# RWKV-7 chain of a decoder step: where its masks are made, and where the next part's transposes and products are issued

## The chip, the core and the metric

The kernel runs on one core of a Trainium2 chip. The metric is the device time of one execution in microseconds. TensorE's clock has two levels, 1.2 and 2.4 GHz; the profile gives the granted clock of a stretch as a share of 2.4 GHz (0.50 is 1.2 GHz).

## The reference

One inference step of a one-layer decoder trunk for 256 prompt tokens and 8 sample tokens: one wide projection, three branches (stick-breaking attention, cross-attention to a memory, RWKV-7 time mixing), their gated sum, a norm, a mixture of 32 experts, a norm. The change touches only the RWKV-7 branch of the prompt. Its state, one 64x64 matrix for each of 8 heads, goes through all 256 tokens:

```
def step(state, inp):
    r_t, d_t, k_t, v_t, kk_t, a_t = inp
    s_a = jnp.einsum('bhvk,bhk->bhv', state, -kk_t)
    state = (state * d_t[:, :, None, :] + s_a[..., None] * (kk_t * a_t)[:, :, None, :]
             + v_t[..., None] * k_t[:, :, None, :])
    return state, jnp.einsum('bhvk,bhk->bhv', state, r_t)
wkv, y = lax.scan(step, wkv0, ...)
```

## The kernel before

One program, written out by hand for each engine; engines meet by semaphores only. SyncE and GpSimd issue DMAs, TensorE multiplies into eight PSUM banks, ScalarE (`move`) and VectorE take results out. `psum_plan` lists in order which named group of matmuls uses which bank. `start(name)` waits on TensorE until the bank's group before has been taken out, `done` says that a group is finished, `take` waits for that on the reader's side, `gone(engine, name)` waits until a group has been taken out. Every engine runs its instructions in program order.

The program has these stages, by the trace: projections, attention and memory branches to about 450 us; the RWKV chain from 486 to 671; output projections, norm and router to about 760; the experts to 1700; the last norm.

The RWKV chain works in 64-token chunks, each turned from a recurrence into products with a triangular inverse. It is cut in four parts, `it` = 0 to 3: two tiles of 128 tokens (`tt`), and in each two halves of the heads (`hh`). A part holds four 128x128 blocks (128x512 in all) and two chunks (`cc`). On TensorE a part is:

- `tab`, `tkv`: 8 transposes, moved out by ScalarE to `tokAB`, `tokKV`
- the products `g1` (two groups, 16 matmul records), `g2` (16), `g3` (8), each of 64 rows of contraction; VectorE takes them out through masks: `g1` to `Nl` (L1805) and `Nt` (L1806), `g2` and `g3` to `RB`, `AK`, `RK` (L1816 to L1819)
- `branches(...)`, steps of matmuls for the other branches' output projections and gates, 22 steps a part, spread by `PLACES`: 4 steps at "start", 2 at each other place, two places of which (U0, U1) lie in the state steps. A group of such steps that is complete is moved out by ScalarE, and of the memory branch gated and summed by GpSimd (`gated`, L650, L651)
- a wait for `T_ready`, that VectorE gives after L1809 to L1812: `Tm` and `Tt` are the first level's mask of `Nl`, `Nt`, plus the identity
- five levels of the inverse: `X` = N'T, moved out by ScalarE; then `TX` and `XT`, which VectorE adds to `Tm` (L1824) and `Tt` (L1827). N' is `Nt` times the level's mask; GpSimd makes all five `Nm[lv]` at the part's start (L674), as soon as both `g1` are taken out
- `MV`, `Z`, `WT`, moved out by ScalarE
- the state steps, for each of two chunks: `U`, added by VectorE (L1837), `dS`, added to the state (L1840) and decayed (L1843) by VectorE, which gives `S_ready` for the next `U`
- `Y`, the part's output, moved out by ScalarE.

All of one part stands ahead of all of the next on every engine. On VectorE a part's order is: g1 masks, T, g2 and g3 masks, levels, state steps. After the four parts come norm, gate and output projection of the branch (L1848 to L1872), and `merged`. The experts' weights come in 192 chunks of 2 MB through six buffers (`pair_loads`): the first six are asked for when the buffers' last users (the last gate, `o`, `merged`, `res`) are done, each later one when TensorE has used the chunk before it in its buffer.

Of the kernel before, what the change touches and what calls it, by code (L numbers as in the profile page):

```python
# [21 lines left out]
P = 128  # L22
# [31 lines left out]
Q0, K0, V0, MQ0, RW0 = 0, 4, 8, 12, 16  # L54

# [15 lines left out]
def beside():  # L71

    g = []
    for kind, br in (("gate", 0), ("o", 0), ("gate", 1), ("o", 1), ("gate", 2)):
# [6 lines left out]
PLACES = {"start": (0, 4), "X0": (4, 6), "X1": (6, 8), "X2": (8, 10), "X3": (10, 12), "X4": (12, 14),  # L81
          "MV": (14, 16), "WT": (16, 18), "U0": (18, 20), "U1": (20, 22)}
# [18 lines left out]
def psum_plan():  # L101
# [61 lines left out]
    for tt in range(2):  # L163
        for hh in range(2):
            n = (tt, hh)
            add(("tab",) + n, six[4])
            add(("tkv",) + n, six[5])
            for hp in range(2):
                add(("g1", hp) + n, six[hp])
            for hp in range(2):  # L170
                add(("g2", hp) + n, six[2 + hp])
            for hp in range(2):
                add(("g3", hp) + n, six[4 + hp])
            for lv in range(5):
                add(("X", lv) + n, six[0])
                if lv < 4:
                    add(("TX", lv) + n, six[1])
                add(("XT", lv) + n, six[2])
            add(("MV",) + n, six[3])
            add(("Z",) + n, six[4])  # L180
            add(("WT",) + n, six[5])
            for cc in range(2):
                add(("U", cc) + n, six[0])
                add(("dS", cc) + n, six[1])
            add(("Y",) + n, six[3])
# [46 lines left out]
def build(nc, A, O):  # L232
# [6 lines left out]
    with ctx:  # L239
# [89 lines left out]
        tokAB, tokKV = ar(R0, 2, 256), ar(R0 + 512, 2, 256)  # L329
        Nl, Nt, Tm, Tt, Xm, AK, RB, RK = (ar(R0 + 1024 + 512 * i, 4, P) for i in range(8))  # L330
        Nm = [ar(R0 + 5120 + 512 * i, 4, P) for i in range(5)]
# [194 lines left out]
        def _(g):  # L526
# [57 lines left out]
            link(g.tensor_tensor(m_lo[:], blk[:], m_upi[:], ALU.subtract))  # L584
            link(g.tensor_scalar(blk64[:], blk[:], 1.0 / 64, 0.0, ALU.mult, ALU.add))
# [83 lines left out]
            for it in range(4):  # L669
                n = (it // 2, it % 2)  # L670
                gone(g, ("g1", 0) + n)
                gone(g, ("g1", 1) + n)
                for lv in range(5):
# [39 lines left out]
        def _(pe):  # L713
# [307 lines left out]
            for tt in range(2):  # L1021
                for hh in range(2):
                    n = (tt, hh)
                    cols = slice(tt * P, tt * P + P)
                    it = 2 * tt + hh
                    tiles = (2 * hh, 2 * hh + 1)
                    if it == 0:
                        pe.wait_ge(sem("hats"), 1)
                    for nm, srcs in (("tab", (KK, AA)), ("tkv", (KM, pT[:, 24:28, :]))):
                        b = start((nm,) + n)  # L1030
                        for i, src in enumerate(srcs):
                            for tl, t in enumerate(tiles):
                                last = tr(b[:, 256 * i + P * tl:256 * i + P * tl + P], src[:, t, cols])
                        done((nm,) + n, last)
                    hats = {"A": KK, "B": AA, "K": KM, "R": pT[:, RW0:RW0 + 4, :]}
                    for nm, prods in (("g1", ("BA", "AB")), ("g2", ("BR", "KA")), ("g3", ("KR",))):
                        for hp in range(2):
                            b = start((nm, hp) + n)
                            rows = slice(64 * hp, 64 * hp + 64)
                            for i, lr in enumerate(prods):  # L1040
                                for tl, t in enumerate(tiles):
                                    c0 = 256 * i + P * tl
                                    last = mm(b[:, c0:c0 + P], hats[lr[0]][rows, t, cols], hats[lr[1]][rows, t, cols], True, True)
                            done((nm, hp) + n, last)

                    branches(*at_place(it, "start"))
                    pe.wait_ge(sem("T_ready"), it + 1)
                    for lv in range(5):
                        if lv:
                            gone(pe, ("TX", lv - 1) + n)  # L1050
                        pe.wait_ge(sem("Nm_ready"), 5 * it + lv + 1)
                        b = start(("X", lv) + n)
                        for u in range(4):
                            last = mm(b[:, u * P:u * P + P], Nm[lv][:, u, :], Tm[:, u, :], True, True)
                        done(("X", lv) + n, last)
                        branches(*at_place(it, f"X{lv}"))
                        if lv:
                            gone(pe, ("XT", lv - 1) + n)
                        gone(pe, ("X", lv) + n)
                        if lv < 4:  # L1060
                            b = start(("TX", lv) + n)
                            for u in range(4):
                                last = mm(b[:, u * P:u * P + P], Tt[:, u, :], Xm[:, u, :], True, True)
                            done(("TX", lv) + n, last)
                        b = start(("XT", lv) + n)
                        for u in range(4):
                            last = mm(b[:, u * P:u * P + P], Xm[:, u, :], Tt[:, u, :], True, True)
                        done(("XT", lv) + n, last)
                    b = start(("MV",) + n)
                    gone(pe, ("tkv",) + n)  # L1070
                    for hp in range(2):
                        gone(pe, ("g2", hp) + n)
                        gone(pe, ("g3", hp) + n)
                    for tl in range(2):
                        for hp in range(2):
                            u, c0 = 2 * hp + tl, 64 * (2 * tl + hp)
                            last = mm(b[:, c0:c0 + 64], AK[:, u, :], tokKV[:, 1, c0:c0 + 64], True, True)
                    done(("MV",) + n, last)
                    branches(*at_place(it, "MV"))
                    gone(pe, ("MV",) + n)  # L1080
                    gone(pe, ("XT", 4) + n)
                    b = start(("Z",) + n)
                    for tl in range(2):
                        for hp in range(2):
                            u, j = 2 * hp + tl, 2 * tl + hp
                            last = mm(b[:, 64 * j:64 * j + 64], Tt[:, u, :], MVs[:, j, :], True, True)
                    done(("Z",) + n, last)
                    b = start(("WT",) + n)
                    for tl in range(2):
                        for hp in range(2):  # L1090
                            u, c0 = 2 * hp + tl, 64 * (2 * tl + hp)
                            last = mm(b[64 * hp:64 * hp + 64, P * tl:P * tl + P], tokAB[:, 0, c0:c0 + 64], Tt[:, u, :], True, True)
                    done(("WT",) + n, last)
                    branches(*at_place(it, "WT"))
                    gone(pe, ("WT",) + n)
                    gone(pe, ("tab",) + n)
                    for cc in range(2):
                        c = 2 * tt + cc
                        rows = slice(64 * cc, 64 * cc + 64)
                        if 2 * it + cc:  # L1100
                            pe.wait_ge(sem("S_ready"), 2 * it + cc)
                        else:
                            pe.wait_ge(sem("S_zero"), 1)
                        b = start(("U", cc) + n)
                        for tl, t in enumerate(tiles):
                            last = mm(b[rows, P * tl:P * tl + P], WTs[:, tl, rows], Sb[c % 3][:, t, :], True, True)
                        done(("U", cc) + n, last)
                        branches(*at_place(it, f"U{cc}"))
                        gone(pe, ("U", cc) + n)
                        b = start(("dS", cc) + n)  # L1110
                        for tl in range(2):
                            o = b[:, P * tl:P * tl + P]
                            uc = Us.rearrange("p a b -> p (a b)")[rows, P * tl:P * tl + P]
# [964 lines left out]
```

## Time and profile before

| | |
|---|---|
| three runs | 1732.66, 1735.74, 1736.46 us |
| median | 1735.74 us |
| the profiled execution | 1734.74 us, its span 1733.1 us |
| TensorE matmuls busy | 1538.8 us, 89% |
| VectorE busy | 596.8 us, 34% |
| ScalarE, GpSimd busy | 280.2 us, 180.5 us |
| granted clock, mean | 0.939 |
| HBM read | 528.91 MB |

The profile is one execution. Its timeline merges neighbouring instructions of one engine and form; the idle time ahead of an instruction and what ended it stand in brackets. Matmuls are pipelined and their ends are modelled, so work is better measured from start to start. A float32 matmul of the program is two matmul records. PE is TensorE, DVE VectorE, ACT ScalarE, POOL GpSimd.

### The profile page before, as it was taken

The numbers are of one execution on the slowest core, as the hardware profiler recorded it, in microseconds if no ns is written. First come the engines' busy times: TensorE is split into PE (matmuls) and PEld (weight loads), VectorE is DVE, ScalarE is ACT, GpSimd is POOL, SyncE is SP. The second block draws the span as 40 slices with busy tenths as digits, with TensorE's granted clock in tenths as the row PEclk, the third lists the DMA queues.
The fourth block names the chain that finished last, engine by engine and source line by source line (L and its number), as shares of the span: only waits on it lengthen the run. The fifth ranks groups of instructions, "written<-read, shape, count | busy, mean of one in ns | idle before, by whom it ended". The sixth has DMA issues, their size and how long they took to land.

```text
span 1733.1 us, 20943 instructions
## 1 busy us (share of the span) xinstructions
PE 1538.8 (89%) x7762; PEld 818.1 (47%) x7762; DVE 596.8 (34%) x888; ACT 280.2 (16%) x538; POOL 180.5 (10%) x290
## 2 busy tenths in 40 slices
PE   7985877778898997969999999999999999999993
PEld 5764533456687775454343434443434333333331
DVE  2699633157634444422121212121212121212125
ACT  1100233113311112110111111111111111011102
POOL 5522131103033112000000000000000000000000
PEclk9998878889988998969999999999999999999997
DMA  8798796766211012439999999999999999999990
GB/s 306 249 326 317 234 306 217 279 249 205 98 25 46 4 50 81 194 126 425 425 429 429 428 428 429 429 429 428 426 429 429 429 429 427 428 429 429 429 425 27
DMA packets 83913, 534.10 MB, mean 308 GB/s; under 512 B 8639, under 2 KB 9722, under 8 KB 59282
## 3 DMA queue, kind: packets, MB, share of 16 engines
q1 hardware_dynamic: 69714, 487.61, 68.7%
q0 software_dynamic: 14144, 45.79, 8.1%
q8 instruction: 31, 0.51, 0.1%
q14 instruction: 24, 0.20, 0.0%
HBM read 528.91 MB, written 4.46 MB: 308 GB/s over the span
## 4 chain that ended last, share of the span: by engine, by line
PE 56%; DMA 26%; DVE 9%; issue 4%; ACT 2%; POOL 1%; POOLq 0%; SPq 0%; DVEq 0%; ACTq 0%
PE bank L728 54%; DMA projT<-in_w_gate_up 23%; PE bank L729 2%; DVE ring L1604 2%; DMA ring<-in_w_in 2%; DMA ring<-in_w_mem_kv 1%; DVE ring L1693 1%; DVE sample_logits L1610 1%; DVE arena L1695 0%; DMA ring<-in_cache_sb_k 0%; DVE arena L1810 0%; DVE arena L1812 0%; DVE arena L1811 0%; ACT arena L1355 0%; DVE arena L2041 0%
## 5 line engine op out<-in xcount | busy, mean ns | idle before, releaser
L728 PE MATMUL bank<-arena 128*128 128x128 f32 (+9 forms) x2172 | 346.4, 364 | 36.9 <-DVE arena L1812 11.2
L728 PEld LDWEIGHTS bank<-arena 128*128 128x128 f32 (+4 forms) x2172 | 238.2, 187 | 153.3 <-issue 127.3
L728 PE MATMUL bank<-ring,memT 128*64 128x512 f32 (+2 forms) x1152 | 282.8, 599 | 8.7 <-ACT memT L1550 7.6
L728 PE MATMUL bank<-projT,ring 128*128 128x264 f32 x1056 | 264.5, 407 | 26.2 <-DMA ring<-in_w_in 17.3
L1981 DVE TENSOR_SCALAR arena<-bank 128x256 f32<-128x256 f32 x64 | 27.0, 422 | 637.6 <-PE bank L728 637.6
L728 PE MATMUL bank<-projT 128*64 128x512 f32 (+1 forms) x1056 | 235.4, 591 | 8.6 <-DMA projT<-in_w_gate_up 8.6
L728 PEld LDWEIGHTS bank<-projT,ring 128*128 128x128 f32 x1056 | 206.3, 200 | 73.0 <-issue 21.6
L728 PE MATMUL bank<-ring,projT 128*64 128x512 f32 x1024 | 230.3, 597 | 0.0
L728 PEld LDWEIGHTS bank<-ring,memT 128*64 128x64 f32 (+2 forms) x1152 | 85.2, 139 | 156.6 <-issue 138.5
L728 PEld LDWEIGHTS bank<-projT 128*64 128x64 f32 (+1 forms) x1056 | 77.1, 141 | 162.2 <-issue 136.8
L728 PEld LDWEIGHTS bank<-ring,projT 128*64 128x64 f32 x1024 | 69.3, 137 | 147.4 <-issue 147.4
L707 POOL DMA_DIRECT2D out_y_sample<-arena x1 | 0.5, 507 | 966.6 <-DVE arena L1892 966.6
L1546 ACT ACTIVATE arena<-arena 128x256 f32<-128x256 f32 x64 | 26.7, 417 | 419.1 <-DVE arena L1981 419.1
L729 PE MATMUL bank<-ident,arena 128*128 128x128 f32 (+4 forms) x386 | 71.3, 304 | 22.9 <-DMA arena<-in_x_sample 8.1
L729 PEld LDWEIGHTS bank<-ident,arena 128*128 128x128 f32 (+4 forms) x386 | 51.7, 171 | 80.0 <-issue 67.0
L1604 DVE TENSOR_TENSOR ring<-ring,bank 128x4096 f32<-128x4096 f32 x16 | 70.6, 4414 | 40.1 <-PE bank L728 20.3
L1355 ACT ACTIVATE arena<-bank 128x512 f32<-128x512 f32 (+7 forms) x98 | 48.0, 513 | 222.9 <-PE bank L728 178.8
L1610 DVE TENSOR_REDUCE sample_logits<-ring 128x64 f32<-128x4096 f32 x16 | 70.7, 4420 | 0.6
L1355 ACT ACTIVATE projT<-bank 128x264 f32<-128x264 f32 (+2 forms) x68 | 26.0, 384 | 239.9 <-PE bank L728 228.4
L1996 DVE TENSOR_TENSOR arena<-arena,bank 128x512 f32<-128x512 f32 x64 | 41.1, 683 | 56.3 <-PE bank L728 56.3
L448 POOL DMA_DIRECT2D ring<-in_cache_sb_k x64 | 34.4, 538 | 109.2 <-issue 89.8
L448 POOL DMA_DIRECT2D ring<-in_cache_sb_v x64 | 34.4, 537 | 94.6 <-issue 94.6
(272 smaller groups left out, 974.0 us busy)
## 6 DMA issues: line engine op xcount, KB each, us to landing
ring<-in_w_gate_up SPq DMA_DIRECT2D x64, 2048.0 KB, 21.2
projT<-in_w_gate_up SPq DMA_DIRECT2D x64, 2048.0 KB, 23.8
ring<-in_w_down SPq DMA_DIRECT2D x64, 2048.0 KB, 20.4
ring<-in_w_in SPq DMA_DIRECT2D x13, 2048.0 KB, 9.1
ring<-in_cache_sb_k SPq DMA_DIRECT2D x64, 256.0 KB, 5.2
ring<-in_cache_sb_k POOLq DMA_DIRECT2D x64, 256.0 KB, 5.9
ring<-in_cache_sb_v SPq DMA_DIRECT2D x64, 256.0 KB, 5.0
ring<-in_cache_sb_v POOLq DMA_DIRECT2D x64, 256.0 KB, 5.3
```

The lines of the kernel that those rows point to most:

```text
L448: eng.dma_start(dst[:, j, :], src[bass.ds(page, 1), :, :].rearrange("g p n -> p (g n)")).then_inc(sem(landed_sem), 16)
L707: g.dma_start(dst, yacc[0:rows, tt, :]).then_inc(sem("out_done"), 16)
L728: mm = lambda out, l, r, first, last, **k: pe.matmul(out, l, r, start=first, stop=last, **k)
L729: tr = lambda out, src, rows=P: pe.transpose(out, src, ident[0:rows, 0:rows])
L1355: act.activation(dst, src_of(b), func, **k).then_inc(freed_by(name), 1)
L1546: act.activation(sg[u % 2], gb[u % 2], ACT.Sigmoid, scale=SWA).then_inc(sem("sg_ready"), 1)
L1604: prod_ = tt_(k, k, q[:, :].unsqueeze(1).to_broadcast([P, 8, W5]), ALU.mult)
L1610: v.tensor_reduce(zs[:, b_, 8 * half:8 * half + 8, :], slot(name).rearrange("p (n h d) -> p n h d", n=8, h=SBH), AX.X, ALU.add).then_inc(s ...
L1693: tt_(k, k, q[:, :].unsqueeze(1).to_broadcast([P, 2, W5]), ALU.mult).then_inc(freed_by(("mqb", b_)), 1)
L1981: ts(g_, chunk[:, 0:512:2], LIMIT, None, ALU.min).then_inc(sem("g_ready"), 1)
L1996: tt_(yacc[:, tt, c], yacc[:, tt, c], bank[b][:, :], ALU.add).then_inc(sem("scatter_added"), 1)
```

## The change

- GpSimd no longer makes `Nm`. VectorE does (`next_level`), one level ahead: level 0's right after `T_ready`, level lv+1's ahead of the TX addition of level lv. Two buffers instead of five.
- `m_lo` is multiplied once by the first level's mask (one more GpSimd instruction of 128x128 among the masks), so that g1's second half goes to `Tm` directly; `Nl` and L1809 go.
- The next part's transposes and its `g1` and `g2` are issued on TensorE between this part's state steps: tab, tkv behind U0, g1 behind dS0, g2 behind U1 and dS1. Only `g3` stays at the part's own start. `tokAB`, `tokKV`, `RB`, `RK` get second buffers, taken in turn.
- ScalarE moves the next part's transposes out ahead of this part's Y.
- VectorE does the next part's g1 masks and T (`first_blocks`) between its addition to U1 and the second state update (`decay_state(1)`); the g2 and g3 masks (`other_products`) come after it.
- The branch steps at U0 and U1 go to "start", which has 8 instead of 4. Banks: g1 in banks 2 and 4, g2 in 5 and 6, g3 in 2 and 4, Y in bank 0.

```diff
-PLACES = {"start": (0, 4), "X0": (4, 6), "X1": (6, 8), "X2": (8, 10), "X3": (10, 12), "X4": (12, 14),
-          "MV": (14, 16), "WT": (16, 18), "U0": (18, 20), "U1": (20, 22)}
+PLACES = {"start": (0, 8), "X0": (8, 10), "X1": (10, 12), "X2": (12, 14), "X3": (14, 16), "X4": (16, 18),
+          "MV": (18, 20), "WT": (20, 22)}
...
+            link(g.tensor_tensor(m_lo[:], m_lo[:], lev[0][:], ALU.mult))
...
-                gone(g, ("g1", 0) + n)
-                gone(g, ("g1", 1) + n)
-                for lv in range(5):
-                    g.tensor_tensor(Nm[lv], Nt, lev[lv + 1][:].unsqueeze(1).to_broadcast([P, 4, P]),
-                                    ALU.mult).then_inc(sem("Nm_ready"), 1)
...
+                ahead = RW_PARTS[it + 1] if it < 3 else None
+                state_in_chunk(0)
+                if ahead:
+                    turned_hats(ahead, "tab")
+                    turned_hats(ahead, "tkv")
+                state_change(0)
+                if ahead:
+                    gram(ahead, "g1", 0)
+                    gram(ahead, "g1", 1)
+                state_in_chunk(1)
+                if ahead:
+                    gram(ahead, "g2", 0)
+                state_change(1)
+                if ahead:
+                    gram(ahead, "g2", 1)
...
+            def next_level(it, lv):
+
+                tt_(Nm[lv % 2], Nt, m4(lev[lv + 1]), ALU.mult).then_inc(sem("Nm_ready"), 1)
...
-                tt_(Tm, Nl, m4(lev[0]), ALU.mult)
                 link(tt_(Tt, Nt, m4(lev[0]), ALU.mult))
                 tt_(Tm, Tm, m4(ident), ALU.add)
                 tt_(Tt, Tt, m4(ident), ALU.add).then_inc(sem("T_ready"), 1)
+                next_level(it, 0)
...
                 for lv in range(5):
                     if lv < 4:
+                        next_level(it, lv + 1)
                         b = take(v, ("TX", lv) + n)
...
+                    if cc == 0:
+                        decay_state(0)
+                if it < 3:
+                    first_blocks(it + 1)
+                decay_state(1)
```

## Rows read from the trace of the kernel before

**Rows 1.** The page, its 40 slices: GB/s moved in each slice of 43.3 us
```profile
GB/s 306 249 326 317 234 306 217 279 249 205 98 25 46 4 50 81 194 126 425 425 429 429 428 428 429 429 429 428 426 429 429 429 429 427 428 429 429 429 425 27
```

**Rows 2.** The chain of waits, ahead of part 3's first level: start us, us, what
```profile
628.68 1.64 DVE arena L1811
630.32 1.68 DVE arena L1812
```

**Rows 3.** Timeline of TensorE, U0 of part 2 to X0 of part 3: start, length, instruction, [idle]
```profile
613.56 0.65 PE L728 MATMUL bank<-arena 128*64 128x128 f32 x4
614.14 1.16 PE L728 MATMUL bank<-projT,ring 128*128 128x264 f32 x4
615.23 1.16 PE L728 MATMUL bank<-arena 64*128 64x128 f32 x8
617.36 0.65 PE L728 MATMUL bank<-arena 128*64 128x128 f32 x4 [0.98 <-DVE arena L1843]
...
622.48 0.88 PE L729 MATMUL bank<-ident,arena 128*128 128x128 f32 x6
...
623.50 1.37 PE L728 MATMUL bank<-arena 64*128 64x128 f32 x13
...
626.70 2.05 PE L728 MATMUL bank<-projT,ring 128*128 128x264 f32 x8
632.04 2.07 PE L728 MATMUL bank<-arena 128*128 128x128 f32 x8 [3.30 <-DVE arena L1812]
```

**Rows 4.** Busy time by stretches: length, engines' busy us, clock (PEclk is the column after POOL)
```profile
520.88:544.40 23.52, 18.84 (x113) 14.91 (x113) 10.57 (x17) 2.36 (x5) 7.20 (x6) 0.76 0.00 1
544.40:569.65 25.25, 25.25 (x164) 22.39 (x164) 8.61 (x17) 4.92 (x10) 6.73 (x8) 0.89 0.24 84
...
588.14:613.56 25.42, 25.42 (x165) 22.62 (x165) 8.61 (x17) 4.53 (x9) 2.31 (x2) 0.88 0.00 1
...
632.04:656.27 24.23, 24.23 (x165) 21.36 (x165) 8.61 (x17) 4.93 (x10) 2.31 (x2) 0.93 0.00 1
656.27:665.20 8.93, 7.95 (x58) 6.00 (x57) 3.03 (x8) 0.39 (x1) 0.00 (x0) 1.00 0.01 2
```

**Rows 5.** Timeline of TensorE, X0 of part 0
```profile
498.17 1.16 PE L728 MATMUL bank<-arena 128*128 128x128 f32 x8 [1.30 <-DVE arena L1812]
```

**Rows 6.** Busy time by stretches of 2 us; the clock is the column after POOL
```profile
528.00:530.00 2.00, 2.00 (x10) 1.78 (x10) 0.52 (x2) 0.00 (x0) 0.00 (x0) 0.50 0.00 0
...
576.00:578.00 2.00, 2.00 (x21) 1.57 (x19) 0.85 (x2) 0.00 (x0) 0.00 (x0) 1.00 0.00 0
...
580.00:582.00 2.00, 2.00 (x30) 2.00 (x30) 1.14 (x4) 0.35 (x1) 0.00 (x0) 1.00 0.04 8
...
588.00:590.00 2.00, 1.86 (x8) 1.86 (x9) 2.00 (x7) 0.00 (x0) 2.00 (x2) 0.50 0.00 0
...
594.00:596.00 2.00, 2.00 (x17) 1.97 (x17) 1.17 (x2) 0.11 (x1) 0.00 (x0) 0.91 0.00 0
```

**Rows 7.** Timeline of VectorE: a level's addition, U's addition, masks
```profile
505.15 0.69 DVE L1824 TENSOR_TENSOR arena<-arena,bank 128x512 f32<-128x512 f32 x1 [2.29 <-PE bank L728]
...
618.12 0.43 DVE L1837 TENSOR_TENSOR arena<-bank,arena 64x256 f32<-64x256 f32 x1 [0.29 <-PE bank L728]
...
626.28 0.69 DVE L1809 TENSOR_TENSOR arena<-arena,lev 128x512 f32<-128x512 f32 x1
...
631.91 0.41 DVE L1816 TENSOR_TENSOR arena<-bank,m_upi 128x256 f32<-128x256 f32 x1
632.24 0.41 DVE L1817 TENSOR_TENSOR arena<-bank,m_up 128x256 f32<-128x256 f32 x1
```

**Rows 8.** Timeline of GpSimd: a gated sum of the memory branch
```profile
504.58 0.75 POOL L650 TENSOR_TENSOR projT<-sample_logits,projT 128x264 f32<-128x264 f32 x1 [2.57 <-ACT sample_logits L1355]
```

**Rows 9.** Timeline of GpSimd: the mask m_lo, among the setup instructions
```profile
60.57 0.46 POOL L584 TENSOR_TENSOR m_lo<-blk,m_upi 128x128 f32<-128x128 f32 x1
```

**Rows 10.** The chain of waits behind GpSimd's masks: the K pages' transfer
```profile
80.89 7.08 DMA ring<-in_cache_sb_k
```

More of the change, by code:

```diff
@@ L162, in psum_plan, with grams @@
             turn += 1
[L163 to L173, printed above, removed]
-            for lv in range(5):
[L175 to L185, printed above, removed]
+    def grams(n):
+        add(("tab",) + n, six[4])
+        add(("tkv",) + n, six[5])
+        for hp in range(2):
+            add(("g1", hp) + n, six[2 + hp])
+        for hp in range(2):
+            add(("g2", hp) + n, six[4 + hp])
+    grams(RW_PARTS[0])
+    for it, n in enumerate(RW_PARTS):
+        for hp in range(2):
+            add(("g3", hp) + n, six[2 + hp])
+        for lv in range(5):
+            add(("X", lv) + n, six[0])
+            if lv < 4:
+                add(("TX", lv) + n, six[1])
+            add(("XT", lv) + n, six[2])
+        add(("MV",) + n, six[3])
+        add(("Z",) + n, six[4])
+        add(("WT",) + n, six[5])
+        if it < 3:
+            grams(RW_PARTS[it + 1])
+        for cc in range(2):
+            add(("U", cc) + n, six[0])
+            add(("dS", cc) + n, six[1])
+        add(("Y",) + n, six[0])
     add("wkv_out", 0)
@@ new lines, in _, with turned_hats, gram @@
+            hats = {"A": KK, "B": AA, "K": KM, "R": pT[:, RW0:RW0 + 4, :]}
+            def turned_hats(n, nm):
+                tt, hh = n
+                b = start((nm,) + n)
+                for i, src in enumerate({"tab": (KK, AA), "tkv": (KM, pT[:, 24:28, :])}[nm]):
+                    for tl in range(2):
+                        last = tr(b[:, 256 * i + P * tl:256 * i + P * tl + P], src[:, 2 * hh + tl, tt * P:tt * P + P])
+                done((nm,) + n, last)
+            def gram(n, nm, hp):
+                tt, hh = n
+                cols = slice(tt * P, tt * P + P)
+                b = start((nm, hp) + n)
+                rows = slice(64 * hp, 64 * hp + 64)
+                for i, lr in enumerate({"g1": ("BA", "AB"), "g2": ("BR", "KA"), "g3": ("KR",)}[nm]):
+                    for tl in range(2):
+                        c0 = 256 * i + P * tl
+                        last = mm(b[:, c0:c0 + P], hats[lr[0]][rows, 2 * hh + tl, cols], hats[lr[1]][rows, 2 * hh + tl, cols], True, True)
+                done((nm, hp) + n, last)
@@ L1097, in _ @@
                     for cc in range(2):
                         c = 2 * tt + cc
[L1099 to L1113, printed above, removed]
-                            mm(o, tokAB[rows, 1, P * tl:P * tl + P], uc, True, False)
-                            last = mm(o, tokKV[rows, 0, P * tl:P * tl + P], tokKV[rows, 1, P * tl:P * tl + P], False, True)
@@ L1128, in _ @@
-                    done(("Y",) + n, last)
+                        mm(b[:, P * tl + 64 * cc:P * tl + 64 * cc + 64], Sb[c % 3][:, t, :],
+                           pT[:, RW0 + t, c * C:c * C + C], cc == 0, True, skip_group_check=True)
+                    for hp in range(2):
+                        u, j = 2 * hp + tl, 2 * tl + hp
+                        o = b[64 * hp:64 * hp + 64, P * tl:P * tl + P]
+                        mm(o, Us[:, j, :], RB[:, u, :], False, True, skip_group_check=True)
+                        last = mm(o, tokKV[:, 1, 64 * j:64 * j + 64], RK[:, u, :], False, True, skip_group_check=True)
@@ L1129, in _ @@
+                done(("Y",) + n, last)
             pe.wait_ge(sem("S_ready"), 8)
@@ L1485, in _, with turned_hats @@
             act.wait_ge(sem("arena_clear"), 2)
[L1486 to L1490 removed]
+            def turned_hats(it):
+                for nm, dst in (("tab", tokABs), ("tkv", tokKVs)):
+                    move((nm,) + RW_PARTS[it], dst[it % 2].rearrange("p a b -> p (a b)"), lambda b: b[:, :])
+            turned_hats(0)
+            for it, n in enumerate(RW_PARTS):
+                tt, hh = n
                 beside_moves(it, "start")
@@ L1797, in _, with first_blocks @@
             m4 = lambda m: m[:].unsqueeze(1).to_broadcast([P, 4, P])
-            for it in range(4):
-                tt, hh = it // 2, it % 2
-                n = (tt, hh)
-                part = lambda b, i: b[:, 256 * i:256 * i + 256].rearrange("p (a b) -> p a b", a=2)
+            part = lambda b, i: b[:, 256 * i:256 * i + 256].rearrange("p (a b) -> p a b", a=2)
+            def next_level(it, lv):
+                tt_(Nm[lv % 2], Nt, m4(lev[lv + 1]), ALU.mult).then_inc(sem("Nm_ready"), 1)
+            def first_blocks(it):
+                n = RW_PARTS[it]
                 for hp in range(2):
```

218 lines of the change are left out of this document (112 added, 106 removed).

## The prediction

> **What bounds the kernel now.** I read the page first, then the chain of waits, then each engine's timeline over the RWKV chain, and last short windows with the clock. The page's line of GB/s [rows 1] shows two kinds of stage: from about 780 us to the end the transfers run flat near 428 GB/s (the experts), before that they don't. The expert stage starts its reloads when TensorE uses a chunk, and each of its first six chunks is asked for when a TensorE or VectorE step ahead of it is done (code of `pair_loads`), so whatever brings the RWKV chain forward should bring the end forward by as much. In the chain of waits around a part's start [rows 2] the path runs through VectorE's two additions of the identity, 1.64 and 1.68 us, and then TensorE's X0.
>
> TensorE's timeline from one part's first state step to the next part's first level [rows 3] shows what is queued: U0 at 613.56, 2 steps of branch matmuls, dS0, U1 after 0.98 us of idle time for the state, the same again, Y, transposes at 622.48, products at 623.50, 4 branch steps at 626.70, and 3.30 us of idle time before X0 at 632.04. The same by stages with the clock [rows 4]: first level to first state step takes 25.25, 25.42 and 24.23 us in parts 1 to 3. In part 0 it takes 22.71 us (498.17 [rows 5] to 520.88 [rows 4]) for the same instructions. The difference (2.5, 2.7, 1.5 us) is clock: right after the 3.3 us of idle time the granted clock is at 0.50, the 1.2 GHz level, and at 594 to 596 is back at 0.91 [rows 6]. So VectorE's preparation costs twice, by idle time and by the slow matmuls behind it.
>
> **Part by part.**
>
> *Transposes, products, branch steps.* Nothing of them is added or dropped (22 branch steps a part as before, now 8 ahead of X0 and none behind U0, U1). What counts is TensorE's own work from U0 to the next X0, at full clock from starts in [rows 3]: U 614.14 - 613.56 = 0.58, twice 1.16; dS: 617.36 - 0.98 - 0.06 of latency - 615.23 = 1.09, twice 2.18; Y: 622.48 - (617.36 + 0.58 + 1.09 + 1.09) = 2.36; transposes 1.02; the five kinds of products 626.70 - 623.50 = 3.20; 8 branch steps 2 x 2.05 = 4.10. Sum 14.02 us. If nothing waits, a part takes 22.71 + 14.02 = 36.73 us, against 43.74 (25.25 from 544.40, 18.49 to 588.14) and 43.90 (25.42 + 18.48) [rows 4].
>
> *Does anything wait?* Count from U0. Transposes end at 1.60. VectorE's addition to U begins 0.76 after the U matmuls begin and takes 0.43 [rows 7], done at 1.2, so dS0 goes at 1.60 and ends at 2.69. VectorE's two state steps and their waits took 1.04 us; S_ready is at 3.73, while the g1 products (16 of the 40 records, 1.28) keep TensorE until 3.97: U1 isn't late, by 0.24. g2 of half a head pair (0.64) ends at 5.19, U's second addition at 5.2: dS1 is on time. Then g2, Y until 9.28. VectorE starts the first blocks at 5.2: four masks at 0.33 [rows 7], then three operations of 128x512 at 0.69 and the first level mask at 0.69: 9.3 with latencies. The second state step follows to 10.2, the six other products (0.33 each) to 12.2, the next level mask to 12.9. X0 is due on TensorE at 14.02, its inputs are there 4.7 us earlier, and its bank (0, now also Y's) is moved out by ScalarE behind Y, while TensorE runs g3 and the branch steps. The decay of chunk 1 now waits behind `first_blocks` on VectorE, but the state it makes is asked for by the next U0, 27 us later, and its bank by TX0, behind X0. The three idle times and the clock loss all go; late next is TensorE itself.
>
> *Masks.* The 20 GpSimd multiplications go, 16 of 20 new ones on VectorE lie inside levels. There VectorE idles 2.29 us before the TX addition [rows 7]. Alone an operation of this shape takes 0.69; beside GpSimd's masks the same shape took 1.64 and 1.68 [rows 2]. GpSimd keeps its gated sums (0.75 each [rows 8]), so I bound the new mask at 0.69 to 1.7 us: below 2.29 either way, cost nothing. The TX addition, which reads PSUM, took 0.69 while GpSimd was busy with such a sum (505.15 [rows 7] against 504.58 to 505.33 [rows 8]), so it stays. The Trainium skill ("SBUF — State Buffer", on the shared port pair) says a VectorE operation with two SBUF inputs is shut out by a GpSimd one that reads SBUF, for a whole instruction, and one with a single SBUF input isn't. The trace agrees with both halves (1.64 against 0.69; 0.69 unmoved). By that rule the new masks can be held for one sum, 0.75 us, which the same idle time covers.
>
> *Part 0's start.* Its X0 comes after 8 instead of 4 branch steps. TensorE had 1.30 us of idle time there [rows 5]; 2.05 us more work brings X0 from 498.17 to 498.92: 0.75 us lost. It gets back below.
>
> *The end of part 3* has no next part to fill in, and U0, U1 have lost their branch steps. U0 0.58, dS0 at 1.24, ends at 2.33, U1 at 3.37, dS1 at 4.61, Y 5.70 to 8.06, against 8.93 [rows 4]: 0.87 gained, and 24.23 - 22.71 = 1.52 of clock ahead of it.
>
> *One GpSimd instruction early on* (m_lo times lev0, about 60 us). Its neighbour took 0.46 [rows 9], 0.52 with its link, and GpSimd's chain there ends in the K page transfers for which VectorE waited (chain of waits, [rows 10]): 0.52 lost, bounds 0 and 0.6.
>
> *Sum.* Part 0: 46.23 (22.71 + 23.52) - 36.73 - 0.75 = 8.75. Part 1: 7.01. Part 2: 7.17. Part 3: 2.39. Together 25.32, less 0.52: 24.8 us. The profiled execution took 1734.74 us (span 1733.1), 1.0 below the median of the three runs: 1709.9 for a like execution, 1711 for the median.
>
> **Rivals.**
>
> *A, the clock falls in the new stretch.* Against the gain speaks part 0 of before: the clock went to 0.50 at 526 and stayed there with TensorE busy 2.00 of 2.00 us (528 to 530, [rows 6]), through dS, Y, transposes and products; U0 to X0 took 23.52 there against 18.49 later. For it speaks the same work at 1.00 at 576 to 578 and 580 to 582 [rows 6], with fewer gaps ahead, and after the change there are none. If it falls once in a boundary, it costs what part 0 shows, 23.52 - 18.49 = 5.0: one boundary gives 1716, three give 1726. The end of part 3 alone, with 2.3 us of idle time in 6, can lose 1.5 to 4: 1713 to 1715. The Trainium skill ("TensorE: Matmul & The Clock Gate", the clock gate) says the default is the slow clock and activity releases it. By that the gapless stretch stays at 2.4 GHz, the forecast; the busy stretch at 528 at 0.50 doesn't agree at once with it.
>
> *B, slower.* The same mechanism carried through: the transposes, 64-row products and state steps in a row hold the clock at 1.2 GHz from U0 to X0 at all three boundaries. Each costs 14.02 more; 42 - 25 makes the kernel 17 us slower, 1736 + 17 = about 1753. It decides at 25.3 / 3 = 8.4 us of full-speed work run at half clock in each boundary. Against it: the rows at 576 and 580, of such work, at 1.00 [rows 6].
>
> *C, no change:* the experts' transfers set the end whatever the chain does. Then 1735 to 1736. Against it: these transfers are asked for by the steps that move.
>
> *D, the overlap fails in part:* U1 waits for the state (slack only 0.24 us) or dS1 for its addition, say 0.5 us each and three times: 1712 to 1714. This lies in the forecast's own range; a full failure (only the masks move, so that 3 x 1 us of slow additions a part go, 12 us with some clock) gives 1722.
>
> **How the numbers follow.** Forecast (1706 to 1716) 0.68; A 0.17; D's full failure 0.05; C 0.04; B 0.06. The range 1705 to 1720 takes in one or two fallen clocks and 2 us each way for the spread of the runs (1732.66 to 1736.46), and leaves out about 2 in 10. About 0.2% (3.5 us) is what a measurement of this kernel can tell from no change. Faster 0.90, same 0.04, slower 0.06.
>
> **What would show it.** Right: no idle time of TensorE ahead of X0 in parts 1 to 3, X0 to X0 near 36.7 us, clock 1.00 from the first X0 to the last U0, the mask lines at 0.69 to 1.7 us ahead of TX additions that still wait for TensorE. Wrong: U1 or dS1 with idle time from VectorE, clock rows at 0.50 between U0 and X0, TX0 waiting for a mask, or an unchanged start of the experts' reloads at an earlier end of the chain.

## The result, and the profile after

The changed kernel took 1710.34 us (median of 4 runs, 1704.75 to 1714.96) against 1736.10 us (4 runs, 1732.66 to 1736.59) for the kernel before: ratio 0.9862, 95% interval 0.9836 to 0.9888. A second set gave 1716.03 us (6 runs, 1707.45 to 1720.16) against 1734.05 us (12 runs, 1723.44 to 1739.21): 0.9882, 0.9862 to 0.9902. So it is 18 to 26 us faster; the forecast was 1711.

| | before | after |
|---|---|---|
| profiled execution | 1734.74 us | 1706.75 us |
| span | 1733.1 us | 1705.0 us |
| TensorE matmuls busy | 1538.8 us | 1527.2 us |
| VectorE busy | 596.8 us | 595.3 us |
| GpSimd busy | 180.5 us | 149.3 us |
| mean granted clock | 0.939 | 0.944 |

First the stretches that answer to [rows 4]: first level to first state step, then first state step to the next part's first level, for parts 0 and 1; then the levels of part 3, and its tail, from U0 to the end of Y. The columns are those of [rows 4]; the clock stands behind POOL.

```profile
493.97:516.30 22.33, 22.33 (x165) 19.80 (x163) 9.31 (x14) 5.71 (x12) 6.49 (x9) 1.00 0.01 1
516.30:530.34 14.04, 14.04 (x114) 12.17 (x114) 10.07 (x23) 2.25 (x5) 1.80 (x3) 1.00 0.00 0
530.34:552.66 22.32, 22.32 (x165) 19.80 (x163) 8.74 (x14) 4.92 (x10) 2.96 (x5) 1.00 0.25 95
552.66:566.70 14.04, 14.04 (x114) 12.17 (x113) 9.62 (x23) 1.86 (x4) 0.00 (x0) 1.00 0.01 1
603.06:625.39 22.33, 22.33 (x165) 19.80 (x163) 8.75 (x14) 4.53 (x9) 0.00 (x0) 1.00 0.00 1
625.39:635.44 10.05, 7.91 (x49) 6.16 (x48) 3.02 (x8) 0.39 (x1) 0.00 (x0) 0.77 0.01 2
```

TensorE is busy all of the first five stretches, at clock 1.00. A part takes 36.36 us (22.32 + 14.04) where it took 43.74 and 43.90. Only the last row has idle time (10.05 - 7.91) and a clock below 1.

The stretch from U0 to X0 of part 1 on TensorE, which answers to [rows 3]:

```profile
516.30 0.65 PE L728 MATMUL bank<-arena 128*64 128x128 f32 x4
516.88 0.87 PE L729 MATMUL bank<-ident,arena 128*128 128x128 f32 x6
...
520.44 0.65 PE L728 MATMUL bank<-arena 128*64 128x128 f32 x4
...
526.67 3.83 PE L728 MATMUL bank<-projT,ring 128*128 128x264 f32 x16
530.34 1.05 PE L728 MATMUL bank<-arena 128*128 128x128 f32 x8
```

and on VectorE, from the first state update to the TX addition of level 1 (L1890 is the decay that ends a state update, L1900 the addition to U, L1850 and L1851 the additions of the identity, L1837 the new level mask, L1876 and L1879 the additions of TX and XT):

```profile
519.55 0.42 DVE L1890 TENSOR_TENSOR arena<-arena 128x256 f32<-128x256 f32 x1
...
521.20 0.43 DVE L1900 TENSOR_TENSOR arena<-bank,arena 64x256 f32<-64x256 f32 x1 [0.70 <-PE bank L728]
...
523.90 0.69 DVE L1850 TENSOR_TENSOR arena<-arena,ident 128x512 f32<-128x512 f32 x1
524.51 0.68 DVE L1851 TENSOR_TENSOR arena<-arena,ident 128x512 f32<-128x512 f32 x1
525.11 0.68 DVE L1837 TENSOR_TENSOR arena<-arena,lev 128x512 f32<-128x512 f32 x1
...
528.62 1.13 DVE L1837 TENSOR_TENSOR arena<-arena,lev 128x512 f32<-128x512 f32 x1
533.27 0.69 DVE L1876 TENSOR_TENSOR arena<-arena,bank 128x512 f32<-128x512 f32 x1 [3.52 <-PE bank L728]
534.24 0.69 DVE L1879 TENSOR_TENSOR arena<-arena,bank 128x512 f32<-128x512 f32 x1 [0.28 <-PE bank L728]
534.96 0.69 DVE L1837 TENSOR_TENSOR arena<-arena,lev 128x512 f32<-128x512 f32 x1
537.07 0.69 DVE L1876 TENSOR_TENSOR arena<-arena,bank 128x512 f32<-128x512 f32 x1 [1.42 <-PE bank L728]
```

The first mask is done at 525.79, 9.5 us behind U0, and X0 starts at 530.34. The additions of the identity take 0.69 and 0.68 us instead of 1.64 and 1.68 [rows 2]. In a level the mask takes 0.69 us out of VectorE's idle time (2.29 [rows 7], now 1.42 left). U1, the row at 520.44, has no idle time ahead of it: its state was done at 519.97. One mask, at 528.62, ran beside two gated sums of GpSimd and took 1.13 us; nobody waited for it.

The tail of part 3 on TensorE, and the clock there in stretches of 2 us:

```profile
625.39 0.65 PE L728 MATMUL bank<-arena 128*64 128x128 f32 x4
626.62 1.16 PE L728 MATMUL bank<-arena 64*128 64x128 f32 x8 [0.58 <-DVE arena L1900]
628.75 0.65 PE L728 MATMUL bank<-arena 128*64 128x128 f32 x4 [0.97 <-DVE arena L1890]
629.99 1.36 PE L728 MATMUL bank<-arena 64*128 64x128 f32 x8 [0.59 <-DVE arena L1900]
...
636.14 1.09 PE L729 MATMUL bank<-ident,arena 128*128 128x128 f32 x4 [0.58 <-ACT arena L1386]
```

```profile
628.00:630.00 2.00, 0.66 (x5) 0.42 (x5) 1.57 (x5) 0.00 (x0) 0.00 (x0) 1.00 0.00 0
630.00:632.00 2.00, 2.00 (x12) 1.77 (x12) 0.58 (x2) 0.00 (x0) 0.00 (x0) 0.70 0.04 8
632.00:634.00 2.00, 2.00 (x13) 1.55 (x13) 0.27 (x1) 0.00 (x0) 0.00 (x0) 0.50 0.00 0
638.00:640.00 2.00, 2.00 (x6) 1.59 (x5) 0.95 (x3) 1.17 (x1) 1.31 (x2) 0.50 0.19 33
```

Three gaps, two of which branch steps used to fill (the one of 0.97, the wait for the state, was there before), then the clock at 0.50 while Y and the first norm products run. The last row of TensorE is a wait that I had not counted: the transposes of `wkv_out` use bank 0, which now also holds Y, and wait 0.58 us until ScalarE has moved Y out.

**A yardstick.** Runs of one kernel lie up to 21 us apart, too wide for terms of 1 to 5 us. The traces are steadier. I measure from X0 of part 0 to the start of the residual's products, the first that need the whole merged tensor. Those rows of TensorE's timeline, before and after:

```profile
702.67 17.55 PE L728 MATMUL bank<-ring,memT 128*8 128x512 f32 x64 [1.12 <-DVEq L1872]
```

```profile
674.86 17.55 PE L728 MATMUL bank<-ring,memT 128*8 128x512 f32 x64 [1.12 <-DVEq L1934]
```

| kernel | X0, part 0 | residual | between | gain | X0 to X0, parts 0, 1, 2 | residual to the span's end |
|---|---|---|---|---|---|---|
| before | 498.17 | 702.67 | 204.50 | | 46.23, 43.74, 43.90 | 1030.4 |
| after | 493.97 | 674.86 | 180.89 | 23.6 | 36.37, 36.36, 36.36 | 1030.1 |
| after, second set | 505.53 | 687.06 | 181.53 | 23.0 | 36.37, 36.37, 36.37 | 1031.3 |
| masks alone | 502.24 | 689.47 | 187.23 | 17.3 | 42.89, 37.85, 37.85 | 1030.5 |
| overlap alone | 503.50 | 685.86 | 182.36 | 22.1 | 36.99, 36.65, 36.65 | 1030.4 |
| tail filled | 502.42 | 680.54 | 178.12 | 26.4 | 36.38, 36.36, 36.37 | 1030.7 |
| steps behind | 497.03 | 669.81 | 172.78 | 31.7 | 34.60, 34.59, 34.59 | 1030.6 |
| no start steps | 497.62 | 669.28 | 171.66 | 32.8 | 34.73, 32.80, 32.82 | 1030.4 |
| overlap and a tiny op | 498.95 | 679.84 | 180.89 | 23.6 | 36.36, 36.37, 36.36 | 1031.1 |

The last column settles one rival: whatever the chain does, the rest takes 1030.1 to 1031.3 us behind it.

The yardstick leaves out part 0's start, where the change costs time. From the first transpose to the residual's products the kernel before took 216.17 us (from 486.50), the changed one 193.64 and 196.24 (from 481.22 and 490.82), the masks alone 196.66 (from 492.81) and the overlap alone 197.04 (from 488.82). Counted so, the gains are 22.5 and 19.9 us for the whole change, 19.5 for the masks alone and 19.1 for the overlap alone. These carry an error that the yardstick hasn't: the granted clock rises from 0.50 to 1.00 within this start, about 9 us behind its beginning before, 6 with the masks alone, 10 and 13 in the two traces of the changed kernel, and the 2.6 us between these two come mostly from that.

### The profile page after: what moved, and what is told of

The parts are those of the page before. It is cut to its first block, busy times and chain, and to the rows that moved or that the text cites. A ratio compares the mean times of both kernels' runs of the same rounds, so it can differ in the third digit from the quotient of the medians.

```text
span 1705.0 us, 20920 instructions
## 1 busy us (share of the span) xinstructions
PE 1527.2 (90%) x7762; PEld 810.9 (48%) x7762; DVE 595.3 (35%) x904; ACT 279.8 (16%) x538; POOL 149.3 (9%) x271
## 4 chain that ended last, share of the span: by engine, by line
PE 58%; DMA 28%; DVE 7%; issue 4%; ACT 2%; POOL 1%; POOLq 0%; SPq 0%; DVEq 0%; ACTq 0%
PE bank L728 56%; DMA projT<-in_w_gate_up 24%; PE bank L729 2%; DMA ring<-in_w_in 2%; DVE ring L1639 1%; DMA ring<-in_cache_sb_k 1%; DMA ring<-in_w_mem_kv 1%; DVE ring L1728 1%; DVE sample_logits L1645 1%; DVE arena L1730 1%; ACT arena L1386 0%; DVE arena L2103 0%; POOLq L452 0%; POOL arena L610 0%; ACT L1427 0%
## 5 line engine op out<-in xcount | busy, mean ns | idle before, releaser
L728 PE MATMUL bank<-arena 128*128 128x128 f32 (+9 forms) x2172 | 335.3, 358 | 23.3 <-DVE arena L1681 8.7
L728 PEld LDWEIGHTS bank<-arena 128*128 128x128 f32 (+4 forms) x2172 | 230.2, 182 | 134.2 <-issue 123.2
L453 POOL DMA_DIRECT2D ring<-in_cache_sb_k x64 | 34.6, 540 | 109.9 <-issue 89.1
L453 POOL DMA_DIRECT2D ring<-in_cache_sb_v x64 | 34.6, 541 | 86.9 <-issue 86.9
```

Source lines behind the costliest of these rows:

```text
L453: eng.dma_start(dst[:, j, :], src[bass.ds(page, 1), :, :].rearrange("g p n -> p (g n)")).then_inc(sem(landed_sem), 16)
L728: mm = lambda out, l, r, first, last, **k: pe.matmul(out, l, r, start=first, stop=last, **k)
```

## Experiments

**The changed kernel again.** No edit.

> The changed kernel itself once more, to see its spread (four runs lay between 1704.75 and 1714.96 us) and a second trace. Theory: the gain is fixed in the RWKV chain, X0 to X0 36.4 us in parts 0 to 3, and the spread comes from ahead of it (the profiled execution reached the chain's first X0 at 493.97 us, before's at 498.17, while the change can only make that 0.75 later): about 1710, same distances inside the chain. Rival: the spread comes from the chain, from a clock that falls in some executions between U0 and X0; then X0 to X0 differs from 36.4 us in a second trace of another total.

1716.03 us. Its chain is the same to 0.01 us a part, with total spans of 1705.0 and 1718.4; X0 of part 0 came at 493.97 and at 505.53. The spread lies ahead of the chain, in code that the change touches by one GpSimd instruction. What moves it there was not followed. The yardstick differs by 0.64 us, nearly all of it behind the last X0: the clock fell again in the tail, but earlier, behind the second of the three gaps (0.97 us, to 640.33) and not behind the third:

```profile
640.00:642.00 2.00, 1.09 (x5) 0.69 (x5) 1.18 (x4) 0.00 (x0) 0.00 (x0) 0.61 0.00 0
```

**Masks alone**, in the kernel before:

```diff
+            link(g.tensor_tensor(m_lo[:], m_lo[:], lev[0][:], ALU.mult))
...
-                for lv in range(5):
-                    g.tensor_tensor(Nm[lv], Nt, lev[lv + 1][:].unsqueeze(1).to_broadcast([P, 4, P]),
...
-                tt_(Tm, Nl, m4(lev[0]), ALU.mult)
...
+                tt_(Nm[0], Nt, m4(lev[1]), ALU.mult).then_inc(sem("Nm_ready"), 1)
...
+                        tt_(Nm[lv + 1], Nt, m4(lev[lv + 2]), ALU.mult).then_inc(sem("Nm_ready"), 1)
```

> The kernel before with the masks alone: VectorE makes them a level ahead, m_lo already has the first level's mask; transposes, products and branch steps stay where they were. Theory (the two halves of the change remove the same idle time and the same clock loss): T is ready 3.0 us sooner, the idle time ahead of X0 falls from 3.30 to about 0.3 us, the clock stays at 1.00 behind it; 5.6 us in each of parts 1 and 2, 3 in part 0 (its clock loss in the state steps stays), 1.5 in part 3, 1.3 at part 0's start, less 0.5: about 1719 to 1720 us. Rival (the halves add, each has its own price): 3 us a part and no clock, 12 us less 0.5: about 1724 us, with clock rows at 0.50 behind X0 as before.

1719.53 us (4 runs; ratio 0.9903, 0.9883 to 0.9924), beside 1734.05 for the kernel before and 1716.03 for the changed one. That is the first theory's number; the rival's gain of 11.5 us (a ratio of 0.9934) lies just outside the interval, and the trace decides. TensorE at X0 of part 1 and part 2, and the stretches from U0 of part 0 and from X0 of part 1:

```profile
545.13 1.13 PE L723 MATMUL bank<-arena 128*128 128x128 f32 x8 [0.26 <-issue]
...
582.98 1.13 PE L723 MATMUL bank<-arena 128*128 128x128 f32 x8 [0.26 <-issue]
```

```profile
524.65:545.13 20.48, 18.85 (x113) 14.94 (x113) 7.53 (x17) 2.36 (x5) 2.00 (x3) 0.75 0.00 0
545.13:567.53 22.40, 22.40 (x164) 19.88 (x164) 11.22 (x21) 4.92 (x10) 4.24 (x6) 1.00 0.25 95
567.53:582.98 15.45, 14.21 (x113) 11.38 (x113) 7.13 (x17) 2.03 (x5) 0.00 (x0) 1.00 0.01 1
```

0.26 us of idle time instead of 3.30, and levels at clock 1.00 where they had 0.88 or 0.89. Part 0's fall in the state steps stays (0.75), as expected. On the yardstick 17.3 of the 23.6 us are there with the masks alone; with part 0's start counted, 19.5 of 19.9 to 22.5, for here that start got shorter (9.43 us instead of 11.67 from the first transpose to X0, in part by a clock that rose earlier), and in the changed kernel longer. By the medians of this set it is 14.5 of 18.0 us.

**Overlap alone**, in the changed kernel, with GpSimd's five masks at the part's start:

```diff
+        Nm += [x[:].rearrange("p (a b) -> p a b", a=4) for x in (w_lora, w_gate2, m_page)]
...
+                for lv in range(5):
+                    g.tensor_tensor(Nm[lv], Nt, lev[lv + 1][:].unsqueeze(1).to_broadcast([P, 4, P]),
+                                    ALU.mult).then_inc(sem("Nm_ready"), 1)
...
-                next_level(it, 0)
...
-                        next_level(it, lv + 1)
```

> The changed kernel, but GpSimd makes all five level masks at the part's start as before (three of the five buffers lie in w_lora, w_gate2s and m_page, which nothing uses by then). Theory: VectorE's three operations of 128x512 in the first blocks cost 1 us more each beside GpSimd, T is ready about 11.7 us behind U0 instead of 8.7, the first mask at about 8.3, and X0 is due only at 14.0: nothing waits, the time is that of the changed kernel, within 2 us. Rival (the halves add): the masks bring 12 of the 25 us, so this one takes about 1722 us and shows idle time ahead of X0.

1716.35 us (4 runs; 0.9874, 0.9845 to 0.9902), 0.3 us from the changed kernel in the same set, on the yardstick 22.1 us. VectorE's first blocks of part 1:

```profile
533.33 0.69 DVE L1851 TENSOR_TENSOR arena<-arena,lev 128x512 f32<-128x512 f32 x1
534.06 1.64 DVE L1852 TENSOR_TENSOR arena<-arena,ident 128x512 f32<-128x512 f32 x1
535.62 1.75 DVE L1853 TENSOR_TENSOR arena<-arena,ident 128x512 f32<-128x512 f32 x1
...
543.50 0.69 DVE L1876 TENSOR_TENSOR arena<-arena,bank 128x512 f32<-128x512 f32 x1 [2.60 <-PE bank L734]
544.39 0.69 DVE L1879 TENSOR_TENSOR arena<-arena,bank 128x512 f32<-128x512 f32 x1 [0.21 <-PE bank L734]
547.37 0.69 DVE L1876 TENSOR_TENSOR arena<-arena,bank 128x512 f32<-128x512 f32 x1 [2.29 <-PE bank L734]
```

The slow additions are back, and X0 of part 1, at 540.49, doesn't wait for them: T is ready at 537.4. So 17.3 + 22.1 is far above 23.6: either half removes nearly the same idle time and clock loss.

**Tail filled**, in the changed kernel:

```diff
+                else:
+                    branches(TAIL, TAIL + 2)
                 state_change(0)
...
-            branches(248, 256)
+            branches(TAIL + 6, 256)
...
-    add("wkv_out", 0)
+    add("wkv_out", 6)
```

> The changed kernel with 6 of the last 8 branch steps moved from behind the chain into part 3's state steps (two behind U0, two behind dS0, two behind U1), and wkv_out in bank 6 instead of 0. In the changed kernel U0 to Y's end took 10.05 us there, with 0.58, 0.97 and 0.59 us of idle time and the clock at 0.50 from 631 to 641, and wkv_out waited 0.58 us for Y's bank. Theory (gaps bring the clock down): no gap, the clock stays at 1.00, U0 to Y's end takes 9.0 us, the first norm products come 1 us sooner and run at full speed: 4 us less, about 1706. Rival (the narrow matmuls of Y and dS bring it down by themselves): the clock falls all the same, gain below 1.5 us.

1711.28 us (4 runs; 0.9858, 0.9839 to 0.9878). The stretches of part 3, its levels and from U0 to Y's end; then two short ones, right behind 1.91 us of idle time between the norm's products, and in the long idle time behind them:

```profile
611.53:633.86 22.33, 22.33 (x165) 19.80 (x163) 8.75 (x14) 4.53 (x9) 0.00 (x0) 1.00 0.00 1
633.86:642.82 8.96, 8.96 (x61) 6.67 (x61) 3.03 (x8) 0.39 (x1) 0.00 (x0) 1.00 0.01 2
...
648.00:650.00 2.00, 2.00 (x11) 1.71 (x10) 0.00 (x0) 1.73 (x4) 0.00 (x0) 1.00 0.00 0
655.00:657.00 2.00, 0.00 (x0) 0.00 (x0) 1.96 (x1) 0.00 (x0) 0.00 (x0) 0.50 0.92 393
```

More work in less time: 8.96 us where 10.05 stood. The same Y and dS, without gaps, ran at 1.00: the narrow matmuls by themselves don't bring the clock down. The filling also put wide matmuls between them, but those aren't needed for it: from U0 to g3 the changed kernel has none (516.30 to 526.67), and that stretch ran at 1.00. Nor does a gap always bring it down: 1.91 us between the wide matmuls of the norm left it at 1.00 (648 to 650). What fell was the clock of narrow matmuls with gaps among them, and not behind each such gap (see the last section).

The runs took 4.75 us less than the changed kernel's in the same set; the yardstick gains 2.8 us (3.4 against the second trace), where I had expected 4. From U0 to the norm's second products 3.6 us were there (13.66 instead of 17.28 us). TensorE then had 11.4 instead of 8.8 us of idle time, and the output projection started at the slow clock as before and stayed there longer: from its start to the residual's products it took 18.64 instead of 17.81 us, 0.8 lost again.

**Steps behind**: the tail filled, and 4 instead of 8 steps ahead of X0; 18 steps instead of 8 behind the norm's last product, and GpSimd gates the sums that they complete there too.

```diff
+PLACES = {"start": (0, 4), "X0": (4, 6), "X1": (6, 8), "X2": (8, 10), "X3": (10, 12), "X4": (12, 14),
+          "MV": (14, 16), "WT": (16, 18)}
...
-GROUP_FIRST, GROUP_STEP = 160, 22
+GROUP_FIRST, GROUP_STEP = 160, 18
...
+TAIL = 232
```

> The kernel with part 3's gaps filled, and 4 instead of 8 branch steps ahead of each X0; the 18 steps left over stand behind the norm's last product (there were 8 in the changed kernel), where TensorE had 8.8 us of idle time and then the branch's output projection at the 1.2 GHz level. Theory (TensorE's own work bounds a part, its inputs at X0 are ready 4.7 us early): X0 to X0 34.3 us in parts 0 to 3 instead of 36.4, no idle time ahead of X0; 8.2 us less in four parts for 6 steps more in the tail that replace its gaps; from the first X0 to the end of the output projection's products 165.9 - 8.2 - up to 2 (clock) = 156 to 158 us, against 168.7 in the changed kernel: the time about 11 us below the changed kernel's. Rival (VectorE bounds X0 once the cover goes): X0 to X0 stays near 36 us with idle time ahead of X0.

1703.12 us (5 runs; 0.9824, 0.9794 to 0.9855). Levels 22.33 us as before, U0 to X0 12.26 instead of 14.04, no idle time at X0. Mine had been 34.3 a part, 34.6 came: I had priced four steps at 2.05 us, the length of their row in [rows 3] (from the first matmul's start to the last one's end, which is more than from start to start); in a row they cost 1.78 (14.04 - 12.26). For that reason and since the clock still fell behind the steps, the yardstick says 172.8, 8.1 below the changed kernel's and not 11.

**No start steps**: as above with none ahead of X0 (14 a part, 34 behind).

```diff
+PLACES = {"start": (0, 0), "X0": (0, 2), "X1": (2, 4), "X2": (4, 6), "X3": (6, 8), "X4": (8, 10),
+          "MV": (10, 12), "WT": (12, 14)}
...
+GROUP_FIRST, GROUP_STEP = 160, 14
...
+TAIL = 216
```

> As the run with the steps behind, but no branch step at all ahead of X0 (14 a part, 34 behind the norm's last product). It measures how much cover X0 has. Theory (from the changed kernel's trace: the first level mask is done 9.5 us behind U0, TensorE gets to X0 at 10.4): still no idle time ahead of X0, X0 to X0 about 32.3 to 32.5 us, at most 0.2 us of waiting for the first TX addition, which stands behind the other six masks; behind the chain the 34 steps take 17.4 us where 12 were idle, so the total is that of the run with the steps behind or up to 3 us above it. Rival (the 4.7 us of cover were not there): idle time of 1 us or more ahead of X0 in each part and a clock at 0.50 behind it, X0 to X0 above 34 us.

1700.18 us (4 runs; 0.9804, 0.9777 to 0.9832). TensorE over part 1, and VectorE at its first level:

```profile
532.35:554.78 22.43, 22.43 (x166) 19.91 (x165) 11.38 (x21) 5.32 (x11) 4.47 (x6) 1.00 0.01 1
554.78:565.15 10.37, 10.37 (x97) 9.02 (x96) 6.99 (x17) 1.86 (x4) 1.49 (x2) 1.00 0.00 0
```

```profile
530.79 0.69 DVE L1845 TENSOR_TENSOR arena<-arena,lev 128x512 f32<-128x512 f32 x1
...
534.30 0.68 DVE L1845 TENSOR_TENSOR arena<-arena,lev 128x512 f32<-128x512 f32 x1
535.39 0.69 DVE L1884 TENSOR_TENSOR arena<-arena,bank 128x512 f32<-128x512 f32 x1 [0.41 <-PE bank L730]
```

U0 to X0 is 10.37 us and still free of waits: the first mask was done at 531.48, 0.9 us ahead of X0 at 532.35, and the TX addition still waits for TensorE, 0.41 us. The cover in the changed kernel was 4.5 us (525.79 to 530.34), where the prediction had counted 4.7. Parts 1 and 2 are 32.8 us long, 0.3 over the forecast. Part 0 is not: it took 34.73 us, because its levels ran partly at the slow clock:

```profile
497.62:521.98 24.36, 24.36 (x165) 21.69 (x165) 11.74 (x21) 5.32 (x11) 4.47 (x6) 0.91 0.00 1
```

With no steps ahead of it X0 came while the clock was still at 0.50, and nearly 2 us of the saving went there (24.36 instead of 22.43 us). The median of the runs is 2.9 us below that of the steps behind, inside the intervals; the yardstick says 1.1.

**No start steps, again:**

> The kernel without branch steps ahead of X0 once more, for an interval beside the kernel before: its chain from the first X0 to the residual's products took 171.7 us against 204.5 before. Theory: ratio 0.981, 32 to 33 us below before. Rival: the last look was a lucky one, 0.985 or above.

1702.47 us (5 runs) against 1731.71 (9 runs): 0.9826, 0.9800 to 0.9852; yardstick 671.62 - 499.96 = 171.66, as in the first trace. It beats the kernel before by its interval and the changed kernel by the yardstick (171.66 against 180.89); between it and the version with 4 steps the runs can't tell.

**Overlap alone, and a tiny VectorE operation in each level:**

```diff
                     if lv < 4:
+                        v.memset(ar(19200, 4), 0.0)
                         b = take(v, ("TX", lv) + n)
```

> The kernel with the overlap alone (GpSimd's masks), plus one tiny VectorE memset (4 elements a row) in each of the first four levels, where the changed kernel has its mask. The levels took 3.80 us each in the changed kernel and with the masks alone, 3.87 us before and with the overlap alone; TensorE's gap ahead of the next X was 0.16 against 0.23 us. Theory: VectorE has two waits ahead of its TX addition (the last addition taken out, TX full), and with an instruction between them each instruction carries one, so that the addition starts 0.07 us sooner: 3.80 us a level here too, the parts 0.3 us shorter than with the overlap alone. Rival: it is GpSimd's work or the place of the buffers: 3.87 us stays.

One run, 1712.51 us. VectorE in a level:

```profile
543.77 0.06 DVE L1875 MEMSET arena<- 128x4 f32 x1
545.85 0.69 DVE L1877 TENSOR_TENSOR arena<-arena,bank 128x512 f32<-128x512 f32 x1 [2.02 <-PE bank L734]
...
547.57 0.06 DVE L1875 MEMSET arena<- 128x4 f32 x1
549.65 0.69 DVE L1877 TENSOR_TENSOR arena<-arena,bank 128x512 f32<-128x512 f32 x1 [2.02 <-PE bank L734]
```

A level takes 3.80 us (549.65 - 545.85), with the overlap alone 3.87 (547.37 - 543.50 above). The whole yardstick is 180.89 us, to the hundredth that of the changed kernel. The rival (GpSimd's work, or the place of the buffers) is refuted. So in this one trace, once the overlap is there, who makes the masks is worth nothing; what the masks still brought was this instruction's place.

## Why the prediction was right, step by step

*What bounds.* Right. TensorE's own work is the limit from U0 to X0: taking 4 and 8 branch steps out shortened it from 14.04 to 12.26 and 10.37 us, without idle time. The rest of the program followed the chain.

*Levels.* I took 22.71 us for every part. 22.33 came: 0.38 less in each of four parts, 1.5 in all. It is the 0.07 us a level above, and 0.10 where X0 begins a part.

*U0 to X0.* 14.02 forecast, 14.04 measured, and that closeness is luck. The 8 branch steps took 3.67 us (526.67 to 530.34) instead of 4.10, and all the rest took 10.37 instead of 9.92, as the run without start steps shows again. The price of the products is what was low: [rows 3] has their 40 records one behind the other in 3.20 us, and the new order pulls them apart. A likely reason, not tested, is that products which contract different halves of the rows start side by side when they are neighbours (pairs at 540.95 and 541.06 in the trace of the masks alone), while the records of one group come 0.11 us apart. There was no wait at U1: its state was done at 519.97, 0.47 us ahead of U1 at 520.44, more than the 0.24 that were counted. At dS1 there was no idle time either, but U's addition was done only at 521.63, when dS1 was due.

*Masks at no cost.* Right, 0.69 us and once 1.13 inside my bounds of 0.69 to 1.7, always ahead of an addition that waits for TensorE. The Trainium skill ("SBUF — State Buffer", "Who interferes with whom") says that a VectorE instruction with two SBUF inputs contends with a GpSimd one that reads SBUF. The overlap alone agrees with it again, 1.64 and 1.75 us beside GpSimd's masks against 0.69 and 0.68 without them.

*Part 0's start.* From the first transpose to X0 took 11.67 us before (486.50 to 498.17), 12.75 after (481.22 to 493.97), 14.71 in the second trace (490.82 to 505.53), where the branch steps ran longer at the slow clock. 0.75 forecast, 1.1 and 3.0 measured: the sign was right and the size depends on when the clock comes back.

*The end of part 3* is the mis-sized term. Forecast: 0.87 gained behind U0 and 1.52 ahead of it. Ahead, 1.90 came (24.23 - 22.33). Behind, from U0 to the residual's products, 46.40 us (656.27 to 702.67) became 49.47 (625.39 to 674.86): 3.1 lost instead of 0.9 gained, 4.0 off. The step that failed is "Y 5.70 to 8.06", which had the idle time right (the gaps were 0.58, 0.97 and 0.59, as worked out) but the matmuls behind it at full clock, and left out the bank of `wkv_out`: Y ended at 10.05, 2.0 later, and the bank cost 0.58. What the sum hadn't looked at, the norm's products behind the transposes, took 5.65 us (637.02 to 642.67) instead of 3.93 before, for the clock was still at 0.50; the projection took 0.6 less than before. Rival A had named and priced this place at 1.5 to 4 us, without being the forecast. Filling it gave 2.8 to 3.4 back.

*The early GpSimd instruction.* It took 0.46 us between neighbours and 0.55 with its link (61.98, 62.52, 63.07). That it moves the end by as much is not shown: the spread ahead of the chain is 20 times larger.

*The sum.* Without part 0's start the forecast for the yardstick was 25.32 + 0.75 = 26.1 us. Plus 1.5 for the levels, less 4.0 for the tail, is 23.6, which is what the trace has. The first set's median fell 25.8 us, the second's 18.0, around that. With part 0's start counted the traces give 22.5 and 19.9. That the first set fits 24.8 so closely is partly luck: two errors of opposite sign, and runs that happened to reach the chain early.

*The rivals.* A happened in the tail only, in none of the three boundaries. B, the slow clock in the dense stretch, didn't happen: five stretches at 1.00 above, and the third boundary too (589.03 to 603.06). The Trainium skill ("TensorE: Matmul & The Clock Gate", "What's actually happening") says that the slow clock is the default and activity releases it. The gapless tail (1.00) and the one with gaps (0.50) agree with it; the stretches at 0.50 in which TensorE was busy 2.00 of 2.00 us (528 to 530 [rows 6], 632 to 634 above) don't at once. C is refuted by the 1030 us. D's full failure is the case of the run with the masks alone. I had priced it at 1722, 12 us with some clock; it measured 1719.5, and its trace has the clock of the levels back as a whole.

## What to carry to other kernels

Where two edits each remove the same wait, their gains don't add: price each against the timeline that the other leaves, and look for a test that has one without the other (here 17.3 and 22.1 us for a pair worth 23.6; with part 0's start counted 19.5 and 19.1 for a pair worth 19.9 to 22.5, so the masks alone, the simpler edit, brought three quarters of the gain or more). Work used as filler in a wait should go where the wait will be afterwards; once the chain fills itself, filler ahead of it is plain load, and here the loop's last turn, which has no next part, was the place that had lost its filler. An idle time of TensorE is to be looked up in the clock rows too: where the granted clock is at 0.50 behind it, as behind the 3.30 us here, it counts twice, by itself and by the matmuls that run at 1.2 GHz; behind 0.26 and 0.98 us it didn't. A yardstick between two points of the trace is to begin ahead of everything that the change moves.

## What the runs showed that I had not expected

- An instruction of VectorE between two waits starts the one behind the second wait sooner: 3.80 against 3.87 us a level, with a mask or with a memset of 0.06 us alike. That each instruction carries one wait and a second one needs an instruction of its own is my explanation; it fits and was not looked at by itself.
- The length of an idle time alone doesn't say whether the clock falls. 0.98 us among the state steps left it at 1.00 in parts 1 to 3 of the kernel before and of the masks alone, and so did 1.30 us ahead of X0 of part 0 [rows 5] and 1.91 us between the norm's products. 1.37 us among the state steps of part 0 brought it down in both kernels, for some 10 us (to 536 us in the kernel before [rows 6], although TensorE was busy). In the unfilled tail (gaps of 0.58, 0.97 and 0.59 us within 5 us) it fell in all four traces, behind the third gap in three and behind the second in one. What decides was not found.
- The same program reached the same instruction at 493.97 and at 505.53 us in two executions, and needed 1030.1 and 1031.3 us for the last 60% of its time. Two traces of it agreed within 0.64 us over the fixed stretch of 181 us, where the intervals of the runs were some 3.5 us each way.
